# Reduced-precision parts for the feature and value projections, swapped operands for the compressed scores, and rotation tables on GpSimd, in a two-layer kernel

## What is computed

```python
kc = compress_kv(k_cmp, cmp_pos_k, cmp_k_w1, cmp_k_w2)        # 31 blocks
s_c = jnp.einsum('bqgrd,bcgd->bqgrc', qb, kc) * scale
p_c = masked_softmax(s_c, m_c)
o_c = jnp.einsum('bqgrc,bcgd->bqgrd', p_c.astype(vc.dtype), vc)
...
return gb[..., 0:1] * o_c + gb[..., 1:2] * o_s + gb[..., 2:3] * o_w
```

## Time and profile before

| | us |
|---|---|
| median of 3 runs | 2035.82 (2035.51 to 2035.95) |
| profiled execution | 2035.84 |
| its span, first to last instruction | 2034.2 |
| PE busy | 1955.2 |
| DVE busy | 930.8 |
| ACT busy | 400.9 |
| POOL busy | 7.5 |

### The profile page before, as it was taken

How to read it: one execution, slowest core, us unless ns; L and a number is a source line. 1 busy time by engine, 2 the same in 40 slices (tenths; PEclk the granted TensorE clock), 3 DMA queues, 4 the chain that set the end, 5 groups by cost and what they waited for, 6 DMA issues and landing times. The chain is left out here.

```text
span 2034.2 us, 25488 instructions
## 1 busy us (share of the span) xinstructions
PE 1955.2 (96%) x9936; PEld 1116.1 (55%) x9937; DVE 930.8 (46%) x1935; ACT 400.9 (20%) x814; POOL 7.5 (0%) x25
## 2 busy tenths in 40 slices
PE   6999999999899999999879999999998999999996
PEld 3458777644644544554434687776454544554542
DVE  7743555342534333443478245553333434433434
ACT  3204444201211111101221044441021111101112
POOL 0000000000000000000000000000000000000000
PEclk9999999999799999999989999999998999999998
DMA  6111111412599999999641012123325999999994
GB/s 246 47 58 63 63 63 56 153 69 104 224 428 428 427 426 427 423 429 421 290 148 47 21 63 83 48 78 124 160 93 233 426 428 423 429 427 424 422 429 172
DMA packets 45259, 484.16 MB, mean 238 GB/s; under 512 B 9456, under 2 KB 9968, under 8 KB 15472
## 3 DMA queue, kind: packets, MB, share of 16 engines
q1 hardware_dynamic: 45168, 482.90, 58.1%
HBM read 476.59 MB, written 6.29 MB: 237 GB/s over the span
## 5 line engine op out<-in xcount | busy, mean ns | idle before, releaser
L1651 DVE TENSOR_TENSOR x_tokens<-x_tokens,ps 128x512 f32<-128x512 f32 x240 | 161.7, 687 | 236.0 <-PE ps L897 234.8
L963 PE MATMUL ps<-arena,branch 128*64 128x512 f32 x512 | 226.6, 595 | 0.0
L963 PE MATMUL ps<-slabs,branch 128*64 128x512 f32 x512 | 226.6, 595 | 0.0
L914 PE MATMUL ps<-arena 128*64 128x512 f32 x512 | 225.1, 592 | 0.0
L913 PE MATMUL ps<-arena 128*64 128x512 f32 x512 | 225.1, 592 | 0.0
L914 PE MATMUL ps<-slabs,arena 128*64 128x512 f32 x512 | 225.0, 592 | 0.0
L913 PE MATMUL ps<-slabs,arena 128*64 128x512 f32 x512 | 224.9, 592 | 0.0
L723 PE MATMUL ps<-h_hi,w_parts 128*128 128x512 f32 x768 | 211.8, 411 | 0.0
L723 PEld LDWEIGHTS ps<-h_hi,w_parts 128*128 128x128 f32 x768 | 139.1, 192 | 36.5 <-issue 10.1
L559 PE MATMUL ps<-slabs,hT 128*128 128x512 f32 x320 | 142.1, 604 | 9.2 <-DVE hT L1246 9.1
L913 PEld LDWEIGHTS ps<-slabs,arena 128*64 128x64 f32 x512 | 70.1, 137 | 146.2 <-issue 146.2
(11 more groups left out here) (333 smaller groups left out, 2733.4 us busy)
## 6 DMA issues: line engine op xcount, KB each, us to landing
arena<-in_expert_w_gate SPq DMA_DIRECT2D x32, 2048.0 KB, 12.0
arena<-in_expert_w_up SPq DMA_DIRECT2D x32, 2048.0 KB, 16.5
arena<-in_expert_w_down SPq DMA_DIRECT2D x32, 2048.0 KB, 9.3
slabs<-in_expert_w_gate SPq DMA_DIRECT2D x32, 2048.0 KB, 15.0
slabs<-in_expert_w_up SPq DMA_DIRECT2D x32, 2048.0 KB, 19.5
slabs<-in_expert_w_down SPq DMA_DIRECT2D x32, 2048.0 KB, 13.8
slabs<-in_dense SPq DMA_DIRECT2D x16, 2048.0 KB, 7.9
slabs<-in_gate_w SPq DMA_DIRECT2D x24, 1024.0 KB, 4.8
```

The costliest lines, as they stand in the source:

```text
L914: return nc.tensor.matmul(ps[64:P, BANK_GU[b], :], xk, high[:, k, :], start=(k == 0), stop=(k == ND - 1), tile_position=(0, 64))
L963: done = nc.tensor.matmul(ps[64 * b:64 * b + 64, BANK_Y[half], :], hidT[:, k, CAP * b:CAP * (b + 1)], w_down[b][:, k, half * 512:(half + 1 ...
L1651: v.tensor_tensor(xs, xs, ps[:, BANK_BACK[n % 2], :], ALU.add).then_inc(s["back_added"], 1)
```

## The change

Slabs: the five f32 slabs of the projections become the gating slab, six halves of 256 columns (state, compressed, keys, two of queries, values) and the compression's slab; the gate slabs keep their form. `S_KS, S_V, S_CMP, S_GATE` are 3, 6, 7 and 8. All ten feature jobs and the four value jobs take the three-part form of the gate jobs. So ACT's high and DVE's low parts of the tokens are made at the layer's start, tile by tile, behind the token job that reads the same tile, and the low weight parts are dealt out over DVE's queue. The gate columns of attention become four jobs of their own between the token jobs. PE's order changes: the four feature jobs of state and compression stand ahead of the transposes of B and the taps, the first key job ahead of the mixing. The residual is read back from the input in layer 0, and saved behind the last additions of layer 0 for layer 1. The rotation tables are made by POOL, and DVE waits for them before the scan. Compressed scores: eight products with the 32 blocks of a group stationary and 512 queries moving, on tiles of 64 rows by 32 columns; DVE and ACT copy one bank each, and eight transposes bring the result into the old form; 8 of the next filling's products stand between.

```diff
-free = {3: (s["proj_done"], J_S5), 4: (s["proj_done"], J_KS), 5: (s["proj_done"], J_KS + 4),
-        6: (s["proj_done"], J_GATE), 7: (s["hidden_done"], 2), S_MIX + 1: (s["outp_done"], ND)}
+free = {3: (s["proj_done"], J_S5), 4: (s["proj_done"], J_KC), 5: (s["proj_done"], J_KS), 6: (s["proj_done"], J_Q),
+        S_CMP: (s["proj_done"], J_Q + 2), 8: (s["proj_done"], J_V), 9: (s["proj_done"], J_GATE),
+        10: (s["hidden_done"], 2), S_MIX + 1: (s["outp_done"], ND)}
...
+    if k == S_CMP:
         sp.wait_ge(s["ysT_done"], 2)
         sp.dma_start(view(O_OACC + 512, 512), row(io["cglu"])[:, 512:1024]).then_inc(s["cglu_in"], 16)
...
+    elif 1 < k < S_CMP:
+        sp.dma_start(half_place(k), half_slab(layer, k)).then_inc(slab_in[k % 3], 16)
+    elif k >= S_CMP:
+        sp.dma_start(view(slab[k % 3], SLAB), io["dense"][layer, 4 if k == S_CMP else k - 15]).then_inc(slab_in[k % 3], 16)
...
-        sp.dma_start(io["x_kept"].rearrange("(t p) d -> p t d", p=P), x).then_inc(s["x_saved"], 16)
...
+        kept = io["x"][0] if layer == 0 else io["x_kept"]
+        sp.dma_start(x, kept.rearrange("(t p) d -> p t d", p=P)).then_inc(s["x_back"], 16)
...
-        sp.dma_start(view(slab[k], SLAB), io["dense"][layer + 1, k]).then_inc(slab_in[k], 16)
+    sp.dma_start(view(slab[0], SLAB), io["dense"][layer + 1, 0]).then_inc(slab_in[0], 16)
+    sp.dma_start(half_place(1), half_slab(layer + 1, 1)).then_inc(slab_in[1], 16)
+    for t in range(NT):
+        sp.wait_ge(s["back_added"], 4 * N_EXP - 8 + 2 * t + 2)
+        sp.dma_start(io["x_kept"][t * P:(t + 1) * P, :], x[:, t, :]).then_inc(x_saved, 16)
...
+def parts_of(k):
+    w = [x[k % 3].rearrange("p (k c) -> p k c", k=ND) for x in (w_hi, w_lo)]
+    return (w[0], h_hi), (w[1], h_hi), (w[0], h_lo)
...
+def halves_ready(m, k):
+    if k == 0:
+        pe.wait_ge(s["w_hi_ready"], m + 1)
+        if m == 0:
+            pe.wait_ge(s["h_hi_ready"], NT)
+    if ND <= k < 2 * ND and (k - ND) % (ND // LO_PIECES) == 0:
+        pe.wait_ge(s["w_lo_ready"], LO_PIECES * m + (k - ND) // (ND // LO_PIECES) + 1)
+    if m == 0 and k == 2 * ND:
+        pe.wait_ge(s["h_lo_ready"], NT)
+def feature_job(n, k0, c):
     out = bank_p(n)
+    for k in range(GATE_MM):
+        halves_ready(k0 - 1, k)
+        w, h = parts_of(k0)[k // ND]
+        last = nc.tensor.matmul(out, w[:, k % ND, c * P:(c + 1) * P], h[:, k % ND, :], start=(k == 0), stop=(k == GATE_MM - 1))
+    last.then_inc(s["proj_done"], 1)
...
+def nsa_job(t):
...
     for k in range(ND):
-        last = nc.tensor.matmul(out, w[:, k, col:col + P], hT[:, k, :], start=(k == 0), stop=(k == ND - 1))
-    last.then_inc(s["proj_done"], 1)
+        last = nc.tensor.matmul(ps[:, BANK_S[0], t * 24:(t + 1) * 24], hT[:, k, t * P:(t + 1) * P], wnsa[:, k, :],
+                                start=(k == 0), stop=(k == ND - 1))
+    last.then_inc(s["nsa_done"], 1)
...
 def value_job(t):
     out = bank_p(J_V + t)
-    for k in range(ND):
-        nc.tensor.matmul(out[:, 0:256], hT[:, k, t * P:(t + 1) * P], W[0][:, k, 256:S], start=(k == 0), stop=(k == ND - 1))
-    for k in range(ND):
-        last = nc.tensor.matmul(out[:, 256:280], hT[:, k, t * P:(t + 1) * P], wnsa[:, k, :],
-                                start=(k == 0), stop=(k == ND - 1))
+    for k in range(GATE_MM):
+        halves_ready(S_V - 1, k)
+        w, h = parts_of(S_V)[k // ND]
+        last = nc.tensor.matmul(out[:, 0:256], h[:, k % ND, t * P:(t + 1) * P], w[:, k % ND, :], start=(k == 0), stop=(k == GATE_MM - 1))
     last.then_inc(s["proj_done"], 1)
...
 for t in range(NT):
     pe.wait_ge(s["hT_ready"], t + 1)
-    token_job(J_SGU + t, W[0], 0, S, t)
...
+    token_job(J_SGU + t, w_sgu, 0, S, t)
+    if t == 1:
+        pe.wait_ge(s["small_in"], 16)
+        nsa_job(0)
+    if t >= 1:
+        nsa_job(t)
+for c in range(2):
+    feature_job(J_S5 + c, 1, c)
+for c in range(2):
+    feature_job(J_KC + c, 2, c)
+pe.wait_ge(s["nsa_read"], 1)
 pe.wait_ge(s["bb_ready"], 1)
 for k in range(TB):
     for J in range(2):
...
-wait_slab(1)
-for c in range(2):
-    feature_job(J_S5 + c, W[1], c * P)
-for c in range(2):
-    feature_job(J_KC + c, W[1], 256 + c * P)
 def s5_input(J):
...
+feature_job(J_KS, S_KS, 0)
 pe.wait_ge(s["vn_ready"], NT)
...
 pe.wait_ge(s["proj_free"], J_S5 + 2)
 for J in range(2):
     s5_input(J)
-wait_slab(2)
...
 fill(FILL[1])
 pe.wait_ge(s["ckv_ready"], 1)
+for r in range(R):
+    for g in range(G):
+        rows = slice(64 * g, 64 * g + 64)
+        last = nc.tensor.matmul(ps[32 * r:32 * r + 32, BANK_O[g], :], k_cmp[rows, g, :], q_plain[rows, r, :],
+                                start=True, stop=True, tile_position=(64 * g, 32 * r))
+last.then_inc(s["csb_done"], 1)
+fill(ND)
+pe.wait_ge(s["csb_read"], 2)
 pe.wait_ge(s["glu_read"], 2)
 for t in range(NT):
-    for h in range(H):
-        col = (t % 2) * 256 + h * 32
-        last = nc.tensor.matmul(ps[:, BANK_S[t // 2], col:col + 32], q_plain[:, h % 4, t * P:(t + 1) * P],
-                                k_cmp[:, h // 4, :], start=True, stop=True)
+    for g in range(G):
+        col = (t % 2) * 256 + g * P
+        last = nc.tensor.transpose(ps[:, BANK_S[t // 2], col:col + P], c_block[:, g, t * P:(t + 1) * P], ident)
 last.then_inc(s["cs_done"], 1)
-fill(FILL[2])
+fill(FILL[2] - ND)
 pe.wait_ge(s["cp_ready"], 1)
...
 nc.scalar.activation(cos1, sincos[3], ACT.Sin).then_inc(s["sincos_ready"], 1)
+def split_hi(k):
+    act.wait_ge(slab_in[k % 3], 16 * (k // 3 + 1))
+    nc.scalar.activation(w_hi[k % 3], view(slab[k % 3], SLAB // 2), ACT.Identity).then_inc(s["w_hi_ready"], 1)
+act.wait_ge(x_saved, 16 * NT * layer)
 for t in range(NT):
     evac(J_SGU + t, [(z[:, t, :], bank(J_SGU + t), ACT.Gelu_apprx_tanh, {})])
+    if t < 2:
+        for u in range(2 * t, 2 * t + 2):
+            act.wait_ge(s["hT_ready"], u + 1)
+            nc.scalar.activation(h_hi[:, :, u * P:(u + 1) * P], hT[:, :, u * P:(u + 1) * P], ACT.Identity).then_inc(s["h_hi_ready"], 1)
+        split_hi(t + 1)
+act.wait_ge(s["nsa_done"], NT)
+nc.scalar.activation(nsa_g.rearrange("p t c -> p (t c)"), ps[:, BANK_S[0], 0:NT * 24], ACT.Tanh, scale=0.5).then_inc(s["nsa_read"], 1)
+act.wait_ge(s["proj_free"], J_SGU + NT)
+for t in range(NT):
+    ins = nc.scalar.activation(vn[:, t, :], z[:, t, 256:512], ACT.Square, accum_out=vsumsq[:, t:t + 1])
...
+s5_evac(0)
+split_hi(S_KS)
+act.wait_ge(s["vvar_ready"], 1)
+nc.scalar.activation(vrstd, vsumsq, ACT.Sqrt).then_inc(s["vsd_ready"], 1)
+s5_evac(1)
+act.wait_ge(s["planes_clear"], 2)
+kc_evac(0)
+split_hi(S_KS + 1)
+kc_evac(1)
 for k in range(TB):
     act.wait_ge(s["bb_done"], k + 1)
     nc.scalar.activation(bbT[:, k].rearrange("p a b c -> p (a b c)"), ps[:, BANK_SCORE[k], :], ACT.Identity)\
       .then_inc(s["bb_evac"], 1)
...
 for i in range(2):
     evac(J_KS + i, [(q_rot[:, i, :], bank(J_KS + i), ACT.Identity, {})])
+    if i == 0:
+        split_hi(S_KS + 2)
 for i in range(4):
     evac(J_Q + i, [(q_plain[:, i, :], bank(J_Q + i), ACT.Identity, dict(scale=DH ** -0.5))])
+    if i == 0:
+        split_hi(S_V)
 for t in range(NT):
-    b = bank(J_V + t)
-    evac(J_V + t, [(v_tok[:, t, :], b[:, 0:256], ACT.Identity, {}),
-                   (nsa_g[:, t, :], b[:, 256:280], ACT.Tanh, dict(scale=0.5))])
...
-split_hi(0)
+    evac(J_V + t, [(v_tok[:, t, :], bank(J_V + t)[:, 0:256], ACT.Identity, {})])
+split_hi(S_GATE)
...
-split_hi(1)
...
+            split_hi(S_GATE + got[0] // 2 + 1)
+gate(1)
+act.wait_ge(s["csb_done"], 1)
+nc.scalar.activation(c_block[:, 1, :], ps[:, BANK_O[1], :], ACT.Identity).then_inc(s["csb_read"], 1)
+split_hi(S_GATE + 1)
 gate(sum(FILL[:2]) // GATE_MM)
...
+def low_tokens(t):
+    dve.wait_ge(s["h_hi_ready"], t + 1)
+    dve.wait_ge(s["proj_done"], J_SGU + t + 1)
+    dve.wait_ge(s["nsa_done"], t + 1)
+    cols = slice(t * P, (t + 1) * P)
+    v.tensor_tensor(h_lo[:, :, cols], hT[:, :, cols], h_hi[:, :, cols], ALU.subtract).then_inc(s["h_lo_ready"], 1)
+lows = [0]
+def split_lo(pieces):
+    for _ in range(pieces):
+        m, i = divmod(lows[0], LO_PIECES)
+        if m >= S_V + N_GH:
+            return
+        k = (m + 1 if m < S_V else m + 2) % 3
+        part = slice(i * LO_COLS, (i + 1) * LO_COLS)
+        dve.wait_ge(s["w_hi_ready"], m + 1)
+        v.tensor_tensor(w_lo[k][:, part], view(slab[k], SLAB // 2)[:, part], w_hi[k][:, part], ALU.subtract)\
+         .then_inc(s["w_lo_ready"], 1)
+        lows[0] += 1
+low_tokens(0)
+low_tokens(1)
+split_lo(LO_PIECES)
+low_tokens(2)
+split_lo(LO_PIECES)
+low_tokens(3)
+dve.wait_ge(s["vsq_ready"], 1)
+tell(v.tensor_scalar(vsumsq, vsumsq, 1.0 / 256, EPS, ALU.mult, ALU.add), "vvar_ready")
 dve.wait_ge(s["cparam_in"], 16)
...
-link(v.memset(tab_re[:, :, 0], 1.0))
-link(v.memset(tab_im[:, :, 0], 0.0))
...
     tell(v.scalar_tensor_tensor(vn[:, t, :], z[:, t, 256:512], vrstd[:, t:t + 1], sgu_g, ALU.mult, ALU.mult), "vn_ready")
+split_lo(LO_PIECES)
+split_lo(LO_PIECES)
 for g in range(SG):
...
+dve.wait_ge(s["tables_ready"], 1)
...
```

(40 more changed lines are left out.)

156 lines of the change are left out of this document (48 added, 108 removed).

## The result

The changed kernel takes 2009.85 us in the median of four runs (2009.47 to 2012.09), the kernel before on the same chip 2035.88 (2035.51 to 2037.81): ratio 0.9871, 95% interval 0.9857 to 0.9885, 26 us faster. The forecast was 2008.5. The profiled execution took 2012.09 us with a span of 2010.4.

What follows compares the result with a forecast made beforehand. PE, busy 96% of the span, was taken as the bound. Layer gains of 32.5 and 31.6 us, less 2 x 15.9 of new waits and 2 x 2.5 of contention, took 27.3 from 2035.8: 2008.5 us, range 2003 to 2014.

Steps and rivals of the forecast that it cites:

- A: Ten feature jobs a layer in three passes, 5.5 us each for 6.9: gain of 14.0 us a layer.
- B: Four value jobs a layer in three passes, 2.8 us each for 3.45: gain of 2.5 us a layer.
- C: 24-column gate products only move, at no cost; wait before the taps and its slow clock go: 6.1 us, 5.2 in layer 1.
- D: Compressed scores: 8 products and 8 transposes replace 32 products, whose slow clock goes too: gain of 9.9 us a layer.
- rival 3: Compressed scores: the eight tiles run one after another, 6.8 us for 1.2, giving 2020 us; chance 0.09.
- E: First key job moved ahead: PE waits for DVE's scan before the products within a block; loss of 7.0 us a layer.
- F: Third reduced gate slab, split by ACT only behind its score copy: PE waits 2.7 us a layer, slow clock taken as 0.
- G: Before the transposes of the compressed probabilities PE waits 4.5 us for DVE's softmax, plus 1.7 of clock: 6.2 us a layer.
- Rival 2: GpSimd and DVE alternate operation by operation; powers of B and tables late, 10 us a layer for 2.5: 2023 us; chance 0.23.
- rival 1: New waits smaller or without slow clock (6.8 us back), contention gives 5 back: 1997 to 2004 us; chance 0.17.
- rival 4: Rotation tables so late that DVE's scan and PE lose more than everything gained, slower than before: 2060 us; chance 0.04.
- rival 5: Three-pass jobs starve on low parts in every slab, so the feature-job gain is absent: 10 to 28 us more; chance 0.04.

Runs made afterwards that it cites:

- run 10: Changed kernel with feature and value jobs back in one full-precision pass, early slabs' low parts left out: 2034.48 us, ratio 0.9979.
- after: The changed kernel itself, against the kernel before: 2009.85 us, ratio 0.9871.
- Run 1: Changed kernel with the first 24-column job moved from behind the second token job to behind the first: 2006.04 us, ratio 0.9833.
- run 2: Changed kernel with the first key job back between the input products and the transposes of the gated rows: 1995.13 us, ratio 0.9793.
- run 7: Changed kernel with the second key job between input products and transposes, the first staying ahead of the row products: 2000.13 us, ratio 0.9819.
- run 6: Changed kernel with the second gate slab's high and low parts and the gating products moved into idle time: 2000.78 us, ratio 0.9816.
- run 3: Changed kernel with ScalarE's high part of the second gate slab taken before the first gate evacuation: 2011.04 us, ratio 0.9851.
- run 5: Changed kernel with the old compressed scores, and ScalarE's high part of the second gate slab ahead of the gate evacuations: 2009.71 us, ratio 0.9866.
- run 4: Changed kernel with the rotation tables made by VectorE behind the powers of C, none by GpSimd: 2041.69 us, ratio 1.0003.
- Run 12: Changed kernel with the eight compressed-score products issued three times, 16 more TensorE products a layer: 2020.78 us, ratio 0.9911.

## Why the prediction was right, and which of its steps were not

The sum said 27.3 us, the runs say 26.0 (0.9857 to 0.9885 of the time before), the spans 23.8. Up to the first scores the sum had 14.1 us for layer 0 and 13.2 for layer 1, and the stages give 11.6 and 10.3.

- **A and B hold.** 1.49 us a feature job for 1.4, 0.57 a value job for 0.6 (run 10 against after).
- **C holds, but not its first sentence.** The wait before the taps and its clock are gone, 5.9 us for 6.1. "Only move: nothing by themselves", said of the 24-column jobs, failed: two of them in a row were followed by slow clock in the profiled execution, 1.7 us in layer 0 and 3.4 in layer 1. Run 1, and the count over all runs given there, show it.
- **D was too large by a double count.** It took 3.4 us of slow clock from a window that begins while the 32-column products still run, and also the 8.6 us which those products took at that clock. The share inside the products, 8.58 less 64 records at the 0.107 us of the prediction, is 1.7 us. Read without it D is 8.58 + 1.85 (the slow job behind) - 1.09 - 0.80 = 8.5 and not 9.9. The tiles did run side by side: 1.09 us where I took 1.2, so rival 3 is out.
- **E** is 4.82 + 3.0 of clock in layer 0 and 4.82 + 1.5 in layer 1: 14.1 together, for 14.0. Runs 2 and 7 take it away.
- **F** is 2.65 for 2.7, but its clock, taken as 0 of a possible 1.7, was 0 in layer 0 and 1.6 us in layer 1; over all kernels that have this wait it was 0 in 4 layers and 1.2 to 1.6 us in 8. **G** is 4.14 + 2.5 and 3.39 + 1.5 us for 6.2 each (the clock's share against L801 to L817 in run 6, 3.08 us). What the prediction did not say is that F and G have one cause, VectorE's queue: runs 3 and 6. D less F and G, as the stage, was forecast at +1.0 us in layer 0 and measured at -1.2; run 5 confirms that the new scores bring nothing in this order of work.
- **GpSimd against VectorE** was taken as 2.5 us a layer and cost PE nothing that the trace shows. The tables took 51 us where I worked out 36, with 14 to spare. VectorE lost 0.1 us where I looked, at the powers of B, and over 7 us where I did not, at the powers of C and the value rows, where there was room. The estimate by the Trainium skill's page "GPSIMD Engine Reference", section "Performance versus the Vector engine", was 1.35 us for the widest operations. In the changed kernel they took 1.11 to 1.62, beside VectorE's work; four of the twelve took 1.11, as my own slope had it. The tables were later than both estimates in part because GpSimd's narrow operations were held up beside VectorE's wide ones (0.37 to 0.65 us for 0.20). Rival 2 (turn by turn) is right for VectorE only beside operations of 256 columns and more. Its own sum was off: 7 us on the powers of B and 5 of late tables are 12 us a layer and not 10, some 2027 and not 2023, still inside the range that it gave. Of rival 1 the part without contention came true and the part without slow clock did not. Rivals 4 and 5 are out, but run 4 shows how near rival 5 was: with the tables on VectorE the low parts are 13 us late.
- **The hand-over** was taken as nothing and gave 3.5 us, for a reason that the change's diff does not show.

So the mechanisms of A to G are right but for C's first sentence, and that the total came out within 1.3 us is in part luck: misses of about the same size stood against each other, 5 us of slow clock behind the pair and 3 of double counting on one side, 5 of contention that PE did not feel and 3.5 at the hand-over on the other. The spans are a further 3.5 us below the sum: 0.6 of it is layer 0's later start and 1.6 the clock behind F in layer 1; the rest is not assigned. The forecast was taken at 0.43 and its own range, 2003 to 2014, holds the result.

## What to carry to other kernels

When a part gets faster on the engine that bounds the kernel, walk the queue of the engine behind it: here 8.5 us of saved products turned into waits, until that queue's own jobs were moved into idle time. A piece of filler work has a use at every place where it can stand, so price the place that it leaves as well as the one that it goes to. In run 7 a second piece of the same length filled both places, by the trace; its time is not told from that of run 2, which filled one. Do not add a window's slow clock to a duration that was itself read inside that window.

## What the runs showed of the hardware that I had not expected

- Two jobs of sixteen 24-column products back to back, 3.5 us, were followed or accompanied by a granted clock of 1.2 GHz in 12 of 20 layers (the pair or the job behind it); one such job, 1.7 us, between token jobs never was in six. In layer 1 the six slow cases are those in which the first two token jobs had already lost 2.9 us or more to the slow clock of the layer's start (16.68 to 16.81 us from start to start for 13.81); the four clean ones had lost at most 2.6. Whether one leads to the other was not tried.
- The place of an instruction fetch can cost 3.5 us at a hand-over: 6.7 to 7.2 us of standstill with an instruction packet in the middle of it, 3.6 to 4.0 without. Run 12 against the changed kernel, one edit, goes from 3.7 to 7.2 us.
- Of GpSimd and VectorE side by side: with operations of 8 columns on both, they took 0.17 us on VectorE as before and 0.20 on GpSimd; with 256 or 512 columns on VectorE and 8 or 32 on GpSimd, VectorE's kept their 0.42 and 0.69 us and GpSimd's took 0.37 to 0.65; with operations of 512 columns on both, VectorE's went from 0.69 to as much as 1.67 us and GpSimd's from 1.11 to as much as 1.62.
- Waits of much the same length differ in what follows them. In the same place (L669) a wait of 3.43 us had no slow clock behind it in one layer of run 10 and 2.8 us of it in the other; the wait of 4.82 us there had 1.3 to 3.0 us of it in all 16 layers that have it; the wait of 2.65 us (F) had none in 4 layers and 1.2 to 1.6 us in 8. A price for slow clock read from a single row can be off by as much.
